# A decoder step with latent attention: rotary queries of all heads projected once, plain queries by pairs, weights loaded a pair ahead

## The reference, cut to what matters

```python
z = x @ w_in                                # 1024 -> 384 + 256 + 32
cq = rms_norm(z[..., :384], q_norm)
ckv = rms_norm(z[..., 384:640], kv_norm)
kr = rope(z[..., 640:], pos)                # one rotary key for all heads
q = (cq @ w_q_up).reshape(B, L, 16, 64 + 32)   # 16 heads: 64 plain, 32 rotary
q_rope = rope(q[..., 64:], pos)
q_lat = einsum('blhn,chn->blhc', q[..., :64], w_uk)
s = (q_lat @ ckv.T + q_rope @ kr.T) * 96 ** -0.5    # causal
o = softmax(s) @ ckv ; v = o @ w_uv ; out = v @ w_o
```

## Time and profile before

| | us |
|---|---|
| median of 3 runs (lowest, highest) | 1309.85 (1309.04, 1310.04) |
| profiled execution | 1309.95 |
| its span, first to last instruction | 1308.1 |
| PE busy | 1291.2, 99% |
| DVE busy | 883.1, 68% |
| ACT busy | 619.3, 47% |
| POOL busy | 278.8, 21% |

### The profile page before, as it was taken

The page is one execution under the profiler, slowest core; times in us unless marked ns, Lnnn a source line. Parts: engine busy times, 40 slices in busy tenths (PEclk is TensorE's granted clock), DMA queues, the critical chain, the costliest instruction groups (busy, mean ns, idle before and its releaser), DMA issues.

```text
span 1308.1 us, 26890 instructions
## 1 busy us (share of the span) xinstructions
PE 1291.2 (99%) x9985; PEld 1216.1 (93%) x9985; DVE 883.1 (68%) x1326; ACT 619.3 (47%) x1061; POOL 278.8 (21%) x391
## 2 busy tenths in 40 slices
PE   9999999999999999999999999999999999999998
PEld 9877777669999999999999899999999999999997
DVE  5767676443877478468864768888784784788746
ACT  4366666332555245145433488864552442444424
POOL 1243322001510000011103415646200100101034
PEclk9999999999999999999999999999999999999999
DMA  7231110342242655557752213223435555577501
GB/s 228 69 111 26 30 30 9 92 136 65 65 128 67 155 130 144 153 118 164 173 173 73 73 37 95 78 66 97 115 84 145 131 137 141 139 169 168 163 31 69
DMA packets 210088, 139.97 MB, mean 107 GB/s; under 512 B 27096, under 2 KB 198701, under 8 KB 210000
## 3 DMA queue, kind: packets, MB, share of 16 engines
q1 hardware_dynamic: 199616, 119.11, 31.8%
q0 software_dynamic: 10384, 19.67, 9.1%
HBM read 116.85 MB, written 3.02 MB: 92 GB/s over the span
## 4 chain that ended last, share of the span: by engine, by line
PE 79%; DVE 7%; ACT 5%; DMA 3%; issue 3%; POOL 2%; SPq 0%; DVEq 0%; POOLq 0%; ACTq 0%
PE ps L699 23%; PE ps L738 21%; PE ps L777 6%; PE ps L842 4%; PE ps L1079 3%; PE ps L1066 3%; DMA raw<-raw 2%; DVE wl L2044 2%; DMA raw<-in_ffn_w_gu 2%; PE ps L1102 1%; PE ps L1152 1%; PE ps L1248 1%; PE ps L1290 1%; PE ps L914 1%; PE ps L1452 1%
## 5 line engine op out<-in xcount | busy, mean ns | idle before, releaser
L738 PE MATMUL ps<-Th,wh 128*128 128x280 f32 x576 | 168.1, 292 | 0.0
L738 PE MATMUL ps<-Th,wl 128*128 128x280 f32 x576 | 167.7, 291 | 0.0
L738 PE MATMUL ps<-Tl,wh 128*128 128x280 f32 x576 | 167.4, 291 | 0.0
L2853 POOL DMA_DIRECT2D raw<-raw x36 | 42.9, 1192 | 531.5 <-DMA raw<-in_ffn_w_gu 531.5
L1540 ACT ACTIVATE wh<-raw 128x2048 fp32r<-128x2048 f32 (+4 forms) x50 | 92.3, 1846 | 122.5 <-PE ps L699 112.7
L2044 DVE TENSOR_TENSOR wl<-raw,wh 128x2048 fp32r<-128x2048 f32 (+4 forms) x50 | 113.2, 2264 | 31.9 <-ACT wh L1540 31.8
L738 PE MATMUL ps<-xl,wh 128*128 128x280 f32 x432 | 126.5, 293 | 0.0
L738 PE MATMUL ps<-xh,wh 128*128 128x280 f32 x432 | 126.2, 292 | 0.1
L738 PE MATMUL ps<-xh,wl 128*128 128x280 f32 x432 | 125.8, 291 | 0.0
L699 PE MATMUL ps<-hh,wh 128*128 128x280 f32 x512 | 108.0, 292 | 1.6 <-DVE wl L2044 1.6
L738 PEld LDWEIGHTS ps<-Th,wh 128*128 128x128 f32 x576 | 108.4, 188 | 0.0
(11 more groups left out here) (442 smaller groups left out, 3650.4 us busy)
## 6 DMA issues: line engine op xcount, KB each, us to landing
raw<-in_ffn_w_gu SPq DMA_DIRECT2D x140, 256.0 KB, 4.7
raw<-in_ffn_w_gu SPq DMA_DIRECT2D x36, 512.0 KB, 4.1
raw<-raw POOLq DMA_DIRECT2D x36, 512.0 KB, 5.1
raw<-in_ffn_w_down SPq DMA_DIRECT2D x48, 256.0 KB, 3.1
raw<-in_lru_w_in SPq DMA_DIRECT2D x16, 512.0 KB, 5.0
Ctok<-in_cache_latent SPq DMA_DIRECT2D x48, 128.0 KB, 2.3
raw<-in_ffn_w_down SPq DMA_DIRECT2D x16, 384.0 KB, 3.8
raw<-in_mla_w_o SPq DMA_DIRECT2D x16, 256.0 KB, 3.7
```

Source lines behind the costliest of these rows:

```text
L738: mm = pe.matmul(bank_of(bank), a, b, start=(k == 0 and m == 0), stop=(k == 3 and m == 2))
L2853: pool.dma_start(quarters(raw[u], 3, 2), quarters(raw[u], 0, 3)[:, 0:3:2, :], accum_op=ALU.add).then_inc(r_out, 16)
```

## The change

The rotary part and the plain part of the queries are projected apart.

- Rotary rows: `rope_queries(g, at)` projects the 32 rotary rows of four heads in one tile of 128, for g = 0 to 3, once, ahead of the first head: 18 matmuls each. ACT and DVE copy them to `ropes[g]` (room in xh, xl and stat). Their weights come in 12 DMAs into the room of Ctok[0]; POOL splits them (128x1536).
- Plain rows: `queries(p, n)` projects two heads in a tile of 128: half 0 at the end of the even head, half 1 in the odd head. ACT reads rows 0 to 63 into Q[0], DVE rows 64 to 127 into Q[1].
- The rotation moves to POOL: rows 64 to 95 of Q are ropes x cos and rows 96 to 127 are ropes x sin, and the key in rows 96 to 127 of K is turned (DVE makes it in eight products instead of four). The sines' table `sines` has its place in the end of Ctok[1], inside `wrh`, and is loaded after the last rotary projection.
- `swap` is gone; query weights are split once per pair (`split_queries`) into one pair of buffers, and SP loads the raw weights of pair p + 2 after the split of pair p.
- `keys(p + 1)` moves in the odd head from behind the last block to behind the tail's scores and two transposes. It needs o_lo of the pair before; DVE now does both parts of `outputs_lo` ahead of the tail's maximum.
- Pages of the cache are loaded at other places of SP's queue; the last three of sequence 1 after the last rotation.

The diff, cut to its core:

```diff
@@ buffers
-        rt = put("rt", [32, 2, T])
+        rt = put("rt", [64, 2, T])
+        wql = place("wql", [P, KQ, P], F32R, raw_at + 4 * (PAGES * KV_R + KQ * P))[0]
+        wqh = place("wqh", [P, KQ, P], F32R, raw_at + 4 * PAGES * KV_R)[0]
+        ropes = [place(f"ropes{g}", [P, T], F32, at)[0] for g, at in enumerate((
+            xh_at + 16 * T, xh_at + 4 * KD * T + 16 * T, xh_at + 20 * T, stat_at + 4 * T))]
+        sines = place("sines", [P, T], F32, rp_at - 4 * T)[0]
+        wr, wrh, wrl = (place(n, [P, 4, KQ, P], dt, at)[0] for n, dt, at in (
+            ("wr", F32, ctok_at), ("wrh", F32R, ctok_at + 4 * PAGES * KV_R), ("wrl", F32R, rp_at)))
@@ SP
             sp.wait_ge(s_xt, 10)
+            for g in range(4):
+                for k in range(KQ):
+                    sp.dma_start(wr[:, g, k, :].rearrange("p (h c) -> p h c", h=4),
...
+            def pair_weights(p):
+
+                sp.wait_ge(wq_sw, 2 * p + 4)
+                for h in range(2 * p + 4, 2 * p + 6):
+                    sp.dma_start(wq[p % 2][:, :, NOPE * (h % 2):NOPE * (h % 2) + NOPE], wqv[:, :, hw * h:hw * h + NOPE]
+                                 ).then_inc(wq_in[p % 2], 16)
+
+            def key_pair(p):
+
+                sp.wait_ge(wt_sum, p)
+                sp.dma_start(wuk[:], wukv[:, :, p * P:p * P + P]).then_inc(wuk_in, 16)
+
+            pair_weights(0)
+            sp.wait_ge(s_zms, 6)
+            sp.dma_start(sines[:], c_trig[2 * P:3 * P, :]).then_inc(pg_in[4], 16)
+            pages_0 = numbers(0)
+            sample_pages(0, pages_0)
+            pair_weights(1)
+            key_pair(1)
...
+            for p in range(4, HEADS // 2):
+                if p < 6:
+                    pages_b = numbers(p - 2)
+                    sample_pages(p - 2, pages_b)
+                    sample_ropes(p - 2, pages_b)
+                if p < HEADS // 2 - 2:
+                    pair_weights(p)
+                key_pair(p)
...
@@ PE
+            def rope_queries(g, at):
+
+                for n in range(2):
+                    for k in range(KQ):
+                        for i, (w, x) in enumerate(((wrh, zqh[k][:]), (wrh, zql[:, k, :]), (wrl, zqh[k][:]))):
+                            mm = pe.matmul(ps[:, 512 * (at + n):512 * (at + n) + TH], w[:, g, k, :], x[:, toks(n)],
+                                           start=(k == 0 and i == 0), stop=(k == KQ - 1 and i == 2))
+                mm.then_inc(s_zms, 1)
...
-                pe.wait_ge(q_act, h + 1)
-                pe.wait_ge(q_dve, h + 1)
+                    pe.wait_ge(q_act, p + 1)
+                    pe.wait_ge(q_dve, p + 1)
+                pe.wait_ge(q_rot, h * 3 + 2)
                 for n, i in enumerate(range(4) if u == 0 else (4, 0, 1, 2, 3)):
                     scores(p, u, i)
-                    if i == 3 and u == 1 and not last:
-                        keys(p + 1)
                     if i == 4:
                         pe.wait_ge(s_lte, 6)
                         turn(p, 0, 0)
                         turn(p, 0, 1)
+                        if not last:
+                            keys(p + 1)
...
-                    if i == 3 and u == 0:
-                        queries(h + 1, v, 0)
-                if not last:
-                    if u == 1:
-                        pe.wait_ge(ql_rd, p + 1)
-                    queries(h + 1, v, 1)
-                else:
+                if u == 0 and more:
+                    queries(p + 1, 0)
+                elif u == 1 and not last:
+                    pe.wait_ge(ql_rd, p + 1)
+                    queries(p + 1, 1)
+                elif last:
                     fill(0, 2)
                     fill(0, 3)
...
+            pe.wait_ge(wq_sw, 2)
+            rope_queries(0, 4)
+            pe.wait_ge(s_ve, 5)
+            pe.wait_ge(s_vd, 5)
+            rope_queries(1, 2)
+            rope_queries(2, 0)
+            pe.wait_ge(s_zroot, 8)
+            rope_queries(3, 4)
+            pe.wait_ge(s_zroot, 9)
             for n in range(2):
-                queries(0, 0, n)
+                queries(0, n)
+            pe.wait_ge(s_zinv, 4)
@@ ACT
-                if not last:
-                    read_q(p + u, v)
+                if u == 1 and not last:
+                    read_q(p + 1)
@@ DVE
-            for n, done in enumerate((s_kr, f0_ok)):
+            for n, (r, at, w) in enumerate(((0, 0, 0), (0, 32, 32), (32, 32, 64), (32, 0, 96))):
                 for h in range(2):
...
                 if u == 1 and above_zero(p):
-                    outputs_lo(h - 2, p - 1, u, 0)
+                    for part in range(2):
+                        outputs_lo(h - 2, p - 1, u, part)
                 for n, i in enumerate(order):
                     top_score(p, u, i)
-                    if i == 4 and above_zero(p):
-                        outputs_lo(h - 2, p - 1, u, 1)
@@ POOL
+            def split_queries(p):
+
+                pool.wait_ge(wq_in[p % 2], 32 * (p // 2) + 32)
+                if p > 0:
+                    pool.wait_ge(q_sum, p)
+                pool.tensor_copy(wqh[:], wq[p % 2][:]).then_inc(wq_sw, 1)
+                pool.wait_ge(wq_sw, 2 * p + 3)
+                pool.tensor_tensor(wql[:], wq[p % 2][:], wqh[:].bitcast(F32), ALU.subtract).then_inc(wq_sw, 1)
...
+            def rotary(h):
+
+                p, u, g, rows = h // 2, h % 2, h // 4, slice(32 * (h % 4), 32 * (h % 4) + 32)
...
+                if p > 0:
+                    pool.wait_ge(sc_sum, scored(p - 1, 1, 3 if u else 4))
...
+                pool.tensor_tensor(Q[u][64:96, :], ropes[g][rows, :], trig[rows, :], ALU.mult).then_inc(q_rot, 1)
+                pool.wait_ge(q_rot, 3 * h + 1)
+                pool.tensor_tensor(Q[u][96:P, :], ropes[g][rows, :], sines[rows, :], ALU.mult).then_inc(q_rot, 1)
+                pool.wait_ge(q_rot, 3 * h + 2)
+                pool.tensor_copy(qrot[64:P, :, h:h + 1, :].rearrange("p b a t -> p b (a t)"),
+                                 Q[u][64:P, NP:T].rearrange("p (b t) -> p b t", t=TS)).then_inc(q_rot, 1)
...
+            pool.wait_ge(in_att, 64)
+            pool.wait_ge(pg_in[4], 16 * 13)
+            rotary(0)
             for t in range(2, 4):
                 rows_out(t)
-            pool.wait_ge(wq_in[0], 32)
-            rotary(0, 0)
-            swap(2, 0)
+            split_queries(1)
+            rotary(1)
             key_weights(1)
             for h in range(1, HEADS):
...
+                more = h % 2 == 0 and h < HEADS - 2
+                if more:
+                    split_queries(h // 2 + 1)
+                if h < HEADS - 1:
+                    rotary(h + 1)
...
+                if more:
                     key_weights(h // 2 + 1)
                 if h < HEADS - 1:
                     pool.wait_ge(o_sum, h * 2)
                     values(h + 1, 1 - h % 2)
```

More of the change, by code:

```diff
@@ L575, in _ @@
             sp.wait_ge(in_pg, 16)
-            for b in range(2):
-                pages_b = numbers(b)
-                sample_pages(b, pages_b)
-                if b == 0:
-                    sample_ropes(0, pages_b)
+            def pair_weights(p):
[3 more added lines that the diff above has]
+                                 ).then_inc(wq_in[p % 2], 16)
@@ new lines, in key_pair @@
+            def key_pair(p):
[8 more added lines that the diff above has]
+            key_pair(1)
+            pages_1 = numbers(1)
+            sample_pages(1, pages_1[0:5])
@@ L596, in _ @@
-            pair_weights(0)
-            sample_pages(3, pages_23[1])
-            sample_ropes(1, numbers(1))
-            with sp.Fori(1, HEADS // 2 - 1) as i:
-                pair_weights(i)
-                sample_ropes(i + 1, numbers(i + 1))
+            for p in range(4, HEADS // 2):
[6 more added lines that the diff above has]
+                key_pair(p)
+                if p >= 6:
+                    for b in (4, 5) if p == 6 else (6, 7):
+                        sample_ropes(b, numbers(b))
@@ L602, in _ @@
+            sp.wait_ge(q_rot, 3 * HEADS)
+            for n in range(5, PAGES):
+                sp.dma_start(Ctok[1][:, n:n + 1, :], cache_latent[0, bass.ds(pages_1[n], 1)].rearrange("a p c -> p a c")
+                             ).then_inc(pg_in[1], 16)
             pages_45 = [numbers(b) for b in (4, 5)]
             sp.wait_ge(sc_sum, 9 * (HEADS // 2))
-            sp.wait_ge(q_rot, HEADS)
-            sp.wait_ge(q_dve, HEADS)
+            sp.wait_ge(q_dve, HEADS // 2)
             sp.wait_ge(ql_sum, HEADS // 2)
@@ L1000, in row_tile @@
                 if t == 0:
[L1001 removed]
+                    pe.wait_ge(s_kr, 2)
                     pe.wait_ge(s_zeps, 2)
@@ L1158, in head @@
                 last = isinstance(h, int) and h == HEADS - 1
+                more = not isinstance(p, int) or p < HEADS // 2 - 1
                 if u == 0:
@@ L1179, in head @@
                         mm.then_inc(wt_sum, 1)
-                    if i == 4:
-                        if last:
-                            fill(0, 0)
```

(29 more changed lines are left out.)

144 lines of the change are left out of this document (70 added, 74 removed).

## The result

| | us |
|---|---|
| median after, 4 runs (lowest, highest) | 1326.17 (1325.27, 1327.42) |
| median before, 4 runs beside them | 1309.94 (1309.04, 1310.64) |
| ratio, 95% interval | 1.0126 (1.0114 to 1.0138) |
| profiled execution after, its span | 1325.27, 1323.4 |
| predicted, range | 1323.6, 1316 to 1332 |

The kernel became slower by 1.26%, 16.2 us, six times the 0.2% that a measurement of this kernel can tell. The direction and the range hold; the forecast was 2.6 us short.

The account below looks back on a forecast made before the run. It took PE and the softmax chain both to be full, the chain within 0.2 to 0.35 us of each head. Start +12.6, six odd heads +0.1, seven even +0.7, last odd +0.3: 1309.95 + 13.7 = 1323.6, range 1316 to 1332.

Parts of the forecast that it names:

- slacks of 0.20 and 0.35: Time in us between the softmax chain's end and the first value product, in even and odd heads before.
- Even head: Gain of 0.20 us from fewer queries, less 0.30 for POOL beside DVE: +0.1 us each, +0.7 for seven.
- The term for POOL at work beside DVE: Even head: two smaller normalisations lengthen ahead of the last maximum, +0.15 us each, +0.3, bounds 0 and 0.8.
- Rival 3: POOL blocks DVE: two normalisations of each even head wait 0.7 us each, +7.7, giving 1331.3; chance 0.10.
- Odd head: Keys moved up: start +0.37 us, end -0.35, together +0.02 each, +0.1 for six odd heads.
- The last odd head: DVE's order changes there too and nothing leaves the end: +0.3 us.
- Start: Start of the attention stage: first scores at 86.0 against 73.82, +12.2 us.
- The wait for the sines: Ahead of the first scores PE waits 2.4 us, since the table is loaded only after the last rotary matmul.
- The rotated keys: Start of the stage: 8 products on DVE instead of 4, +0.5 us on the chain, bounds 0 and 1.2.
- 1 (PE is the bound, 1305.8): All 1.16 us come off each head, giving 1305.8; chance 0.10 in full, 0.06 in a weaker form.
- 2 (rotation late): POOL's rotation or the key weights come late, so each odd head starts late: 1330.6; chance 0.08.
- 4: The start overlaps better (table lands sooner, DVE's extra products hide): 2 us less, 1321.6; within the forecast's own range.

Follow-up runs that it names:

- e1: Kernel before with 8 of 9 matmuls of each second half of queries left out in 15 heads (120 matmuls): 1308.93 us, ratio 0.9996.
- e4: Kernel after with POOL's two rotary products cut from 560 to 32 columns for heads 2 to 15: 1324.44 us, ratio 1.0119.
- e5: Kernel after with ACT's copy of the next keys moved from behind the odd head's last exponential to behind its first: 1322.89 us, ratio 1.0110.
- e7: Kernel after with 64 of the 72 rotary projection matmuls left out: 1319.58 us, ratio 1.0079.
- e9: Kernel after with 18 thrown-away matmuls ahead of the first scores and 14 in the last even head's pause: 1327.28 us.
- e10: Kernel after with sines loaded early, K copied early, even heads' outputs_lo behind the last maximum, 14 thrown-away matmuls, two queues reordered: 1321.13 us, ratio 1.0091.
- e11: e10 with 64 of the 72 rotary projection matmuls left out: 1313.86 us, ratio 1.0032.
- e12: e11 with row tile 2's write back ahead of POOL's second split and the next key weights loaded ahead of the pages: 1310.03 us, ratio 1.0008.
- e2: Kernel after with the sines' table in its own room, loaded with the rotary weights: 1327.33 us, ratio 1.0142.

## Why the prediction was right, and where its sizes were off

**The bound of the heads: right, for a partly wrong number.** That the softmax chain decides, in spite of PE's 99%, carried the sign of the forecast, and e1 shows it. But I read slacks of 0.20 and 0.35 from the earlier trace rows by taking 0.06 us for the hand-over from ACT to PE, for which I had no row. Where PE waits, the time from the end of ACT's PT copy to the first value product is 151.89 - (151.06 + 0.59) = 0.24 us in the even head, 143.58 - (142.65 + 0.58) = 0.35 in the odd one, and 0.34 in e1's odd heads. Before, the same distances were 0.26 and 0.40. So the slack was 0.02 and 0.05: PE's work ended with the chain, and there was next to nothing to take (0.11 a pair in e1).

**Even head, +0.1 forecast, +0.26 measured.** The term for POOL at work beside DVE was right: +0.30 at the last maximum (4.49 us from the head's start against 4.19), from 0.29 to 0.45 for the first normalisation (the two lines below, before and after) and 0.35 to 0.70 for the second; e4 takes the second back. The slack of 0.20 that should have paid for it wasn't there.

```profile
133.75 0.29 DVE L2187 TENSOR_SCALAR Pr<-Pr,rsum 128x128 f32<-128x128 f32 x1
...
147.10 0.45 DVE L2241 TENSOR_SCALAR Pr<-Pr,rsum 128x128 f32<-128x128 f32 x1
```

The Trainium skill, page "SBUF — State Buffer", section "Who interferes with whom", says that when VectorE is in its two-port mode, the later of it and GpSimd blocks fully until the other's instruction ends. The row of 0.70 starts at 148.46, inside a product that ends at 149.00, and ends at 149.16; blocked until 149.00 it would have ended at 149.35. The lengthening agrees in kind and is smaller than the rule. No row says in which mode the normalisation ran, and e4 shows that POOL's products slow it, not that the port does. Rival 3, at 0.7 for each of two normalisations, falls: they lost 0.16 and 0.35.

**Odd head, +0.02 forecast, +0.21 measured.** Its start cost 0.45 (the next scores stand at 3.26 us from the tail's scores, against 2.81) where I had 0.37. Its end gave 0.22 (3.02 us from the last scores' end to the value products against 3.24) where I had 0.35: 0.05 of slack, and 0.17 by which the PT copy ends sooner behind those scores (2.67 us instead of 2.84), where I had written that it wouldn't move. K's copy, which in before started on ACT and DVE at once (128.58) when the keys were done, no longer waits for them. What I passed over is that K's copy still stood in the ACT queue inside the chain, where the keys' new place had made it needless; I had taken the queue "as before" and stopped there. e5 shows it to be worth 0.49 a pair, the cheapest mend of all. Odd and even head together, six pairs: 2.5 us where the sum had 0.7. The last odd head, for which the sum had another 0.3, cost nothing: from head 15 on the two kernels take the same time.

**Start: +12.2 forecast, +11.8 measured, by compensation in part.** 72 rotary matmuls at 0.129: right in kind (e7: 7.1 for 64). The wait for the sines: 2.64 against 2.4, released by POOL as said. The rotated keys were to cost 0.5 and cost nothing: keys(0) starts 42.24 us after the input's arrival before and 42.25 after. DVE's split behind the rotation, 2.20 in the earlier trace rows, took 1.43, and an idle time behind it took up the rest. Before, POOL made a subtraction of 1.55 us beside it; now it makes these two, and it is they that are long (0.24 and 0.51 in before, with DVE idle beside them):

```profile
54.75 1.43 DVE L2211 TENSOR_TENSOR xl<-z,xh 128x560 fp32r<-128x560 f32 x2
...
54.79 0.81 POOL L2780 COPY zn<-z 128x64 f32<-128x64 f32 x1 [6.47 <-DVE krs L2206]
...
55.62 0.93 POOL L2801 CAST wqh<-wq 128x384 fp32r<-128x384 f32 x1
```

Head 1 was to be at +12.25 and is at +12.5; head 3 at +12.7 and is at +13.3. That keys(1) were to start at 94.9 and start at 94.92 is luck: the input came 0.5 us sooner in this execution, and counted from its arrival they were to start at 68.3 and start at 68.9.

**The sum.** Forecast: 13.7. Measured from the input's arrival: 12.5 to head 1, 15.8 at head 15 and at the end. The range held, but the term of the pairs is a third of what they cost: 1.8 us too small; 0.3 at head 1 and 0.3 between it and head 3 are missing too, and the last odd head's 0.3 was too much. The spans differ by 15.3, since the input came 0.5 us sooner in the execution of after. Of the 16.2 us between the medians, 0.9 lies between the profiled execution of after, with its clock of 1.00, and the median; whether that is the clock, e9 couldn't show.

**Rivals.** 1 (PE is the bound, 1305.8) fell by e1, and by a pair of 20.14 us instead of 18.5. 2 (rotation late) appeared only where the forecast had it, at head 1 (1.1 us): no later odd head waits for POOL; a product takes 1.37 where I had taken 1.38. 3 fell as told. 4 fell: the table landed as forecast (2.8 us from its issue against 2.7), and DVE's products cost nothing where I had 0.5, which is not 2.

## What to carry to other kernels

An engine that is 99% busy may still not be the bound: look at the chain that ends beside it, and take the hand-over from a place where the engine really waits before calling the rest slack. Work that fills a wait in a loop is free there, and costs its full time where it is gathered ahead of the loop. When a step is moved up, move its readers too, and follow every queue that the moved instructions stand in; an instruction moved back may free a buffer that somebody needs.

## What the hardware showed

- The granted clock fell to its lower level (0.50, that is 1.2 GHz instead of 2.4) within stretches of 6 to 9 us at the end of pauses of PE and behind them, pauses of 1.9 to 3.1 us, in some executions and not in others with the same pause: behind the 2.6 to 2.7 us pause in four profiles of seven, behind the one of 1.8 to 2.3 in three of seven, and behind e10's of 3.1 and e11's of 2.1. Pauses of 0.9 to 1.6 us, thirteen of them in a row in after, never lowered it in a profile. With the long pauses filled (e9) all four runs had 0.999. In e12 the longest pause is 1.3 us and its profile shows no fall while PE works; but three of its eleven runs have 0.998 and took 1311.95 to 1312.31 us, the other eight 0.999 and 1309.32 to 1310.30. What happened in the three isn't known, as none of them was profiled. The group of four matmuls behind the fall took 1.90 us in e2 where it takes 1.04. The Trainium skill, page "TensorE: Matmul & The Clock Gate", section "What's actually happening", says that the throttled state is the default, which activity releases, and that the point of this release varies between runs of one kernel. No run here shows either by itself: what varies here is whether the clock falls behind a pause.
- A product on POOL over 32 partitions took as long as one over 128: 1.37 us for 32x560 in after against 1.38 for 128x560.
- Where DVE and POOL instructions overlapped, either could be the one that lost: DVE's normalisation of 256 columns took 0.70 us beside POOL's product instead of 0.35, and POOL's copy of 128x64 took 0.81 beside DVE's split instead of 0.24.
